# Four constant products on TensorE in each of two pauses of a 256-token network kernel

## The reference, cut to what matters

```
def even_layer(x, ...):                       # layer 0
    h = rms_norm(x, norm_g)
    a_u, a_v, a_g, b_q, b_k, b_v, b_g, m_q, m_g = split_cols(h @ w_in, EVEN_SPLITS)
    y_a = chunked_sgu(gelu(a_u), gelu(a_v), a_ws, a_bs, a_vnorm) * silu(a_g)
    ...                                       # y_b: differential attention, y_m: memory attention
    return x + concatenate([y_a, y_b, y_m]) @ w_out

def odd_layer(x, ...):                        # layer 1
    ...                                       # y_c: a convolution of 31 taps
    y_d = nsa(d_q, kv, gates, pos, ...) * silu(d_g)
    ...
def nsa(...):
    kc = compress(k_cmp_raw, cmp_idx, cmp_pos_k, cmp_w1_k, cmp_w2_k)
    kc = rope_partial(rms_norm(kc, knorm), cmp_end)      # 15 compressed keys of each group
    ...                                       # three attentions: compressed, selected, window
```

## Time and profile before

| | us |
|---|---|
| median of 3 runs | 931.94 |
| lowest, highest of them | 930.04, 932.48 |
| the profiled execution | 932.02 |
| its span, first to last instruction | 930.2 |
| TensorE busy in the span | 889.6 (96%) |
| VectorE, ScalarE, GpSimd busy | 587.6, 389.7, 103.2 |
| mean granted clock of TensorE | 0.992 |

### The profile page before, as it was taken

The page is one execution under the profiler, slowest core; times in us unless marked ns, Lnnn a source line. Parts: engine busy times, 40 slices in busy tenths (PEclk is TensorE's granted clock), DMA queues, the critical chain, the costliest instruction groups (busy, mean ns, idle before and its releaser), DMA issues.

```text
span 930.2 us, 15618 instructions
## 1 busy us (share of the span) xinstructions
PE 889.6 (96%) x6262; PEld 824.1 (89%) x6262; DVE 587.6 (63%) x1114; ACT 389.7 (42%) x703; POOL 103.2 (11%) x114
## 2 busy tenths in 40 slices
PE   6999999999999999999999999999999999999996
PEld 6998988788888777878899999999998999999994
DVE  4784686432788788721597458955665676676673
ACT  6456654012002155612445676445354344543451
POOL 0149660101011000200400000100000000000000
PEclk9999999999999899999999999999999999999999
DMA  9444323243433611140655243555453456645641
GB/s 368 162 176 137 94 89 113 114 159 116 176 138 137 268 50 46 47 151 1 227 172 191 91 136 137 181 185 177 159 188 115 147 169 220 206 157 183 223 140 46
DMA packets 37784, 139.38 MB, mean 150 GB/s; under 512 B 4304, under 2 KB 4432, under 8 KB 37456
## 3 DMA queue, kind: packets, MB, share of 16 engines
q1 hardware_dynamic: 37424, 136.90, 42.5%
q10 hardware_dynamic: 288, 1.48, 0.5%
HBM read 137.32 MB, written 1.05 MB: 149 GB/s over the span
## 4 chain that ended last, share of the span: by engine, by line
PE 79%; issue 8%; DVE 8%; ACT 3%; POOL 1%; DMA 1%; DVEq 0%; SPq 0%; ACTq 0%; POOLq 0%
PE psum L534 18%; PE psum L535 18%; PE psum L536 18%; PE psum L537 18%; PE psum L609 1%; PE psum L667 1%; PE psum L685 1%; ACT logits L1195 1%; PE psum L810 1%; DVE neg_max L1803 1%; DVE psum L1797 1%; PE psum L678 1%; POOL w_lo L2253 1%; DVE rows L1834 1%; DMA rows<-in_mem 1%
## 5 line engine op out<-in xcount | busy, mean ns | idle before, releaser
L1546 DVE TENSOR_TENSOR w_lo<-raw,w_hi 128x1024 fp32r<-128x1024 f32 x162 | 190.9, 1222 | 76.4 <-ACT w_hi L1107 75.5
L534 PE MATMUL psum<-first 128*128 128x256 f32 (+1 forms) x960 | 218.6, 385 | 4.9 <-ACT first L1145 2.2
L534 PEld LDWEIGHTS psum<-first 128*128 128x128 f32 x960 | 180.5, 194 | 31.2 <-ACT first L1145 2.8
L1107 ACT ACTIVATE w_hi<-raw 128x1024 fp32r<-128x1024 f32 x184 | 185.8, 1053 | 34.5 <-PE psum L537 26.2
L535 PE MATMUL psum<-h_hi,w_hi 128*128 128x256 f32 x704 | 199.5, 283 | 0.6 <-issue 0.6
L537 PE MATMUL psum<-h_hi,w_lo 128*128 128x256 f32 x704 | 199.2, 283 | 0.0
L536 PE MATMUL psum<-h_lo,w_hi 128*128 128x256 f32 x704 | 199.2, 283 | 0.0
L535 PEld LDWEIGHTS psum<-h_hi,w_hi 128*128 128x128 f32 x704 | 135.1, 192 | 1.6 <-issue 1.4
L536 PEld LDWEIGHTS psum<-h_lo,w_hi 128*128 128x128 f32 x704 | 135.1, 192 | 0.2
L537 PEld LDWEIGHTS psum<-h_hi,w_lo 128*128 128x128 f32 x704 | 135.1, 192 | 0.0
L535 PE MATMUL psum<-w_hi,h_hi 128*128 128x256 f32 x448 | 129.5, 289 | 0.0
(11 more groups left out here) (268 smaller groups left out, 1071.5 us busy)
## 6 DMA issues: line engine op xcount, KB each, us to landing
raw<-in_blocks SPq DMA_DIRECT2D x184, 512.0 KB, 4.2
first<-in_blocks SPq DMA_DIRECT2D x64, 512.0 KB, 4.5
w_late<-in_blocks SPq DMA_DIRECT2D x4, 512.0 KB, 5.7
early<-in_early SPq DMA_DIRECT2D x1, 1579.0 KB, 16.4
attention<-in_late ACTq DMA_DIRECT2D x1, 1376.0 KB, 6.7
rows<-in_mem SPq DMA_DIRECT2D x2, 512.0 KB, 4.3
x<-in_x SPq DMA_DIRECT2D x1, 1024.0 KB, 8.4
out_x<-h_rows SPq DMA_DIRECT2D x2, 512.0 KB, 2.6
```

The costliest lines, as they stand in the source:

```text
L534: return nc.tensor.matmul(out, lhs[0], rhs[0], start=start, stop=stop, skip_group_check=shared_bank)
L1107: nc.scalar.activation(split_part(w_hi, q), raw[:, q % RAW_SLOTS, :], ACT.Copy).then_inc(w_hi_ready, 1)
L1546: V.tensor_tensor(split_part(w_lo, q), raw[:, q % RAW_SLOTS, :], split_part(w_hi, q).bitcast(F32), ALU.subtract).then_inc(w_lo_vector, 1)
```

## The change

Two calls of `keep_clock` are added, four products each. The first stands behind the transposes of the memory attention's rows and before the wait for the gated rows; it writes to the PSUM slot that the output projection's first part will use. The second stands behind the transposes of the compressed keys and before the wait for their copy; it writes to the slot of the first scores of layer 1.

```
             normed.wait(pe, "y_m0")
             turn_pair("ym0", lambda a, t: rows[:, t, 3840 + a * P:3840 + (a + 1) * P])
+            keep_clock(proj, PROJ_BANK, ("out0", 0), 4)
             normed.wait(pe, "y_a0")
...
             fill(xpose, mm, "kc")
+            keep_clock(score, SCORE_BANK, len(UNITS0), 4)
             turned(pe, "dq0", "dq1", "mk1", "dk0", "dk1", "kc", "mq1")
```

## The result

The changed kernel is slower by a little: median 933.91 us of 20 runs (931.77 to 937.14) against 931.75 of 20 (929.40 to 933.60) on the same chips; the ratio is 1.0022, with a 95% interval of 1.0012 to 1.0031. I had forecast 929.2, and a range that ended at 931.9.

A forecast was written before the change was run, and what follows sets the result against it. TensorE, busy 889.6 of 930.2 us, was taken as the bound, with half clock behind two pauses to win back. 932.02 - 1.69 (first pause) - 1.15 (second) = 929.18, forecast 929.2 us, range 928.4 to 931.9.

The forecast's parts named there:

- The first pause: Layer 0, before the gated rows' transposes: four products fit the pause at no cost and save 1.69 us of half clock.
- Does the gain last?: Between the pauses TensorE sets the pace nearly throughout, so everything up to 317.68 moves up by 1.69 us.
- The second pause: Layer 1, before the first scores: gain 1.24 us, less 0.09 us of products beyond the pause, net 1.15 us.
- The clock still falls at the second pause: Rival, layer 1: thin products bring the clock down, constant products run at half clock, scores 1.82 us later; 931.5 us, chance 0.22.
- A fall elsewhere: Rival: with work 1.7 us earlier, another pause, such as near 342, brings the clock down; costs 1.69 us, 930.9, chance 0.16.
- TensorE's remaining lead is lost in its waits: Layer 1, after the second scores: VectorE sets the pace, so TensorE's further lead adds nothing to the 1.24 us gain.
- The rule weighed against the trace: Falls vary between executions, so the gain against the median is smaller than the 929.2 sum from one trace.

The follow-up runs named there:

- after: Trace of the changed kernel itself, both groups of four constant products added to the kernel before; profiled execution 934.07 us, median 933.91 us, ratio 1.0022.
- first_only_a: Kernel before plus only the four constant products in layer 0's pause; 931.84 us, ratio 1.0003.
- both_thin_a: Kernel before plus both groups, each product with 16 columns instead of 256; 930.36 us, ratio 0.9995.
- first_later: Kernel before plus the first group and four constant products in the wait near 341, none in layer 1's pause; 931.93 us, ratio 0.9998.
- first_x1: Kernel before plus the first group and two constant products in the pause near 220; 932.86 us, ratio 1.0011.
- second_two: Kernel before plus only the second group, with two products instead of four; 932.23 us, ratio 1.0009.
- second_later: Kernel before plus the second group of four and six constant products in the wait near 341; 932.85 us, ratio 1.0011.
- wide_only: Kernel before without constant products, its 16 thin products computed over the full 256 columns; 933.13 us, one run.
- thin_first: Kernel before without constant products, the two halves of dkv2 exchanged so the 24-column products come first; ratio 1.0067.
- second_only_a: Kernel before plus only the four constant products in layer 1's pause; 933.20 us, ratio 1.0019.
- both_again_a: The changed kernel once more, both groups against the kernel before, for a second trace and times; 934.22 us, ratio 1.0025.
- second_wide: Kernel before plus the second group, with the 16 thin products before it computed over the full 256 columns; 937.25 us, one run.
- second_one: Kernel before plus only the second group, with one product instead of four; 930.37 us, ratio 0.9995.
- thin_first_later: Kernel before with the halves of dkv2 exchanged, 24-column products first, and six constant products in the wait near 341; ratio 1.0052.
- first_x1_later: Kernel before plus the first group, two constant products near 220 and four in the wait near 341; 929.40 us, ratio 0.9982.

## Why the prediction was wrong, point by point

- *The first pause: right in place and size, wrong in what remains of it.* 80 records in 17.43 us, 1.69 us saved as worked out, at no cost. "Does the gain last?" is the first step that failed: I followed the chain of waits and not the clock. In the changed kernel's trace the clock falls near 220 instead, and from the transposes ahead of that pause to those of the keys it takes 315.43 - 216.34 = 99.09 us, before 317.39 - 219.97 = 97.42: 1.67 us given back. Of the six traces with a first group and an unfilled pause near 220, four have such a fall (after, first_only_a, both_thin_a, first_later); of the ten without a first group none has. The first group alone is worth nothing that can be told (1.0003), and only with the pauses near 220 and near 341 filled as well is it in a kernel that wins; with that near 220 alone it is slower (first_x1, 1.0011).
- *Why the clock falls near 220 stays open.* That TensorE comes there 1.7 us earlier, with no fall behind it, is not enough. In second_two, second_later, wide_only and thin_first the first pause brought no fall though nothing filled it; they came to the pause near 220 as early as the changed kernel does (51.3 us after the transposes behind the first pause, before 53.0), and none fell there. Nor does it take wide constant products: both_thin_a fell there, and its 16-column products had left TensorE idle for 1.09 us of the first pause. Four of six against none of four can still be chance from execution to execution.
- *The second pause: the step that failed most.* The forecast took the constant products at 0.216 us each. They ran largely at half clock in all four traces with four of them behind thin products (after, second_only_a, both_again_a, second_later), and the scores came 1.36 to 1.87 us later instead of 0.09 (3.29, 3.40, 3.76 and 3.80 us behind the transposes, before 1.93). VectorE lost 0.70 us where I had it gain 1.15. The size of the gain was right for the case that did not happen: where the clock is full to the end of the scores (wide_only), the distance is 1.16 us shorter.
- *The rival "The clock still falls at the second pause" was the truth*, by all signs for the reason given (32 thin records before it), and with nearly the right overrun (1.82 us against 1.4 to 1.9). I gave it 0.22, because in the profiled execution the clock held until 318.4, behind the thin products. That was one execution: the fall starts up to 0.9 us before the transposes in others. The rival's time, 931.5, was too low because it kept the first pause's 1.69 us and left out what follows. *The rival "A fall elsewhere"* came true in the same runs: it named the pause near 342, where the clock did fall. I had priced the two one at a time.
- *"TensorE's remaining lead is lost in its waits" was taken to cost nothing.* In the changed kernel that lead (0.45 us) and VectorE's delay (0.69 us) made the wait near 341 2.7 instead of 1.6 us long, and behind that the clock fell; in second_two and first_x1 the lead alone did it. In all seven traces in which this wait is over 2 us (after, second_only_a, both_again_a, first_x1, second_two, second_wide, thin_first) there is a fall near it; in the five with 1.6 us (before, first_only_a, both_thin_a, second_one, wide_only) and the six with the wait filled there is none. It costs 1.0 to 2.6 us.
- *The rule weighed against the trace.* By the Trainium skill (TensorE: Matmul & The Clock Gate, Part 1: The HAM clock gate) slow products differ in number from execution to execution of one kernel. The traces bear it out: the first 32 records of line 534 take 7.1 us in ten traces and 8.8 to 9.5 in the other eight, and of ten traces without a first group the first pause was followed by a fall in six. By these ten, filling it is worth at most 1.69 us in six of ten executions, some 1.0 us on the average (an estimate). I made it a reason for a smaller gain; it should have been a reason not to take where the clock stood in one trace as where it stands.
- *The sum of it.* Second group: 0.7 of overrun and 1.0 or more of the later fall, 1.7 to 2, where 1.15 were to be won; first group: 0, where 1.69 were to be won. Measured: 1.8 us for the second alone (0.19%), 2.1 for both (0.22%). The fall near 368 in the changed kernel's trace is in second_only_a and thin_first_later too, but not in both_again_a; how much of the difference between executions it makes stays open.

## What to carry to other kernels

Constant products should fit their pause at half clock, not only at full: before adding them, ask what TensorE did just ahead of the pause, and if that was thin products, as here, count on half clock. Even that may not be enough: two products, only 0.3 us too long, hardly delayed VectorE, and yet gave TensorE a lead that became a longer wait. A pause is not one place: a kernel that gains a microsecond comes to the next pause at another time, or waits longer there, and the clock may fall there instead, so fill the pauses behind as well and judge by the time of many runs. Where another engine sets the pace behind the pause, TensorE's clock is worth little there.

## What the runs showed of the hardware that I had not expected

- Products of 24 columns, back to back (32 records in 3.6 us, without idle time), were followed by the lower clock in all 13 traces, in two of them before TensorE had paused at all (in first_x1_later at 313.3, 0.9 us before the transposes). A busy engine in the profile is not one that keeps its clock.
- The first products take a time that differs between executions: the 32 records at 10.7 us took 9.07 us in the trace before and 7.15 in that of the changed kernel, which alone puts the two spans 1.9 us apart. In the trace before, those from 11.30 to 14.29 stand 0.43 us apart, as at half clock elsewhere; in the changed kernel's they stand 0.216 us apart. The column of the granted clock reads 1.00 in both, so that so near the start the spacing of the products tells more than the column:

```profile
10.74 9.07 PE L534 MATMUL psum<-first 128*128 128x256 f32 x32 [1.08 <-ACT first L1145]
11.00:14.00 3.00, 3.00 (x8) 2.38 (x8) 0.17 (x1) 2.30 (x4) 0.17 (x1) 1.00 1.01 404
```

```profile
10.69 7.15 PE L534 MATMUL psum<-first 128*128 128x256 f32 x32 [1.09 <-ACT first L1147]
11.00:14.00 3.00, 3.00 (x15) 2.64 (x14) 0.17 (x1) 2.30 (x4) 0.00 (x0) 1.00 1.03 411
```

- Executions of one kernel are spread over steps of about 2 us (before: 929.4 to 930.5, 931.3 to 932.5, 933.5). One fall more or less (1.7 us) or the start just shown (1.9 us) would each make such a step; which it is was not shown.
